# State space part: turning rows of X and B during the projection that forms them, with all copies on ScalarE

## What is computed

```python
xbc = silu(causal_dwconv(xbc, conv_w, conv_b))        # 4 taps, 4096 columns of h @ w_in
xs, Bm, Cm = split(xbc, (D_INNER, D_INNER + G * N))   # 2048 | 1024 | 1024 columns
dt = softplus(dt_raw + dt_bias)
X = xs * dt[..., None]
a_cs = cumsum(dt * A)
CB = einsum('bclgn,bcsgn->bcgls', Cc, Bc)
y_diag = einsum('bcgkls,bcsgkp->bclgkp', CB * Ldec, X)
states = einsum('bclgn,bcgkl,bclgkp->bcgkpn', Bc, exp(a_cs[..., -1:] - a_cs), X)
y_off = einsum('bclgn,bcgkpn,bcgkl->bclgkp', Cc, prev, exp(a_cs))
y = y_diag + y_off + d_skip[:, None] * xs
```

## Time and profile before

| | us |
|---|---|
| Median of 3 runs | 2085.98 |
| Lowest and highest | 2085.65 and 2087.79 |
| The profiled execution | 2083.6 |
| Its span in the profile | 2081.8 |
| TensorE busy | 1980.2 (95%) |
| VectorE busy | 1660.5 (80%) |
| ScalarE busy | 1303.8 (63%) |
| DMA | 498.76 MB, mean 240 GB/s |

### The profile page before, as it was taken

One profiled execution on the slowest core, in us unless ns is written; L12 is line 12 of the kernel. 1 busy time (PEld: TensorE's weight loads), 2 busy tenths in 40 slices (PEclk: granted clock), 3 DMA queues, 4 the chain that ended last, 5 costly groups with the idle time before them and its releaser, 6 DMA issues. The chain is left out here.

```text
span 2081.8 us, 28079 instructions
## 1 busy us (share of the span) xinstructions
PE 1980.2 (95%) x11165; PEld 1704.3 (82%) x11165; DVE 1660.5 (80%) x2110; ACT 1303.8 (63%) x1943; POOL 0.2 (0%) x4
## 2 busy tenths in 40 slices
PE   7879999998999999999999999989999999999999
PEld 4768788877778888888888888879888789989997
DVE  5876898677689989998999899978755756757884
ACT  3644444366587777787878787757564745536663
POOL 0000000000000000000000000000000000000000
PEclk9888999999999999999999999999999999989999
DMA  8625798731269989998999899845424443324553
GB/s 322 230 101 183 268 366 336 265 147 41 102 261 367 357 334 360 363 363 324 370 357 361 332 365 363 337 166 199 143 81 140 148 160 124 120 99 143 186 187 113
DMA packets 70809, 498.76 MB, mean 240 GB/s; under 512 B 8080, under 2 KB 8336, under 8 KB 11408
## 3 DMA queue, kind: packets, MB, share of 16 engines
q1 hardware_dynamic: 69952, 494.28, 64.1%
q10 hardware_dynamic: 720, 2.62, 0.3%
HBM read 495.82 MB, written 1.05 MB: 239 GB/s over the span
## 5 line engine op out<-in xcount | busy, mean ns | idle before, releaser
L345 DVE TENSOR_TENSOR wlo<-ring,whi 128x1024 fp32r<-128x1024 f32 (+1 forms) x845 | 1016.2, 1217 | 244.1 <-ACT whi L393 223.5
L393 ACT ACTIVATE whi<-ring 128x1024 fp32r<-128x1024 f32 (+1 forms) x845 | 884.8, 1054 | 480.8 <-PE ps L237 402.9
L237 PE MATMUL ps<-whi,hT 128*128 128x256 f32 (+2 forms) x944 | 318.0, 337 | 13.0 <-DVE hTl L299 4.3
L237 PE MATMUL ps<-wlo,hT 128*128 128x256 f32 (+2 forms) x944 | 312.8, 331 | 0.0
L237 PE MATMUL ps<-whi,hTl 128*128 128x256 f32 (+2 forms) x944 | 312.7, 331 | 0.0
L237 PE MATMUL ps<-whi,xg 128*128 128x512 f32 (+1 forms) x768 | 289.3, 377 | 1.4 <-DVE wlo L345 1.1
L237 PE MATMUL ps<-whi,xgl 128*128 128x512 f32 (+1 forms) x768 | 285.8, 372 | 0.0
L237 PE MATMUL ps<-wlo,xg 128*128 128x512 f32 (+1 forms) x768 | 285.5, 372 | 0.0
L237 PE MATMUL ps<-whi,hf 128*128 128x512 f32 x528 | 208.2, 394 | 4.8 <-DVE wlo L345 3.2
L237 PEld LDWEIGHTS ps<-whi,hT 128*128 128x128 f32 x944 | 183.3, 194 | 35.1 <-DVE wlo L345 7.4
L237 PE MATMUL ps<-wlo,hf 128*128 128x512 f32 x528 | 205.7, 390 | 0.0
(11 more groups left out here) (299 smaller groups left out, 2602.8 us busy)
## 6 DMA issues: line engine op xcount, KB each, us to landing
ring<-in_wstream SPq DMA_DIRECT2D x462, 1024.0 KB, 5.0
ring<-in_wstream SPq DMA_DIRECT2D x4, 832.0 KB, 5.2
modrow<-in_gates ACTq DMA_DIRECT2D x3, 512.0 KB, 6.9
ring<-in_wstream SPq DMA_DIRECT2D x6, 256.0 KB, 2.6
cst<-in_cst SPq DMA_DIRECT2D x1, 1028.0 KB, 7.7
x<-in_x SPq DMA_DIRECT2D x1, 1024.0 KB, 13.6
work<-in_bias ACTq DMA_DIRECT2D x2, 512.0 KB, 5.2
ring<-in_wstream SPq DMA_DIRECT2D x2, 512.0 KB, 3.8
```

Of the source, the lines that this page charges most:

```text
L237: i = self.e.matmul(out, lhsT, rhs, start=start, stop=stop, skip_group_check=True)
L345: i = self.e.tensor_tensor(K.wlo[:, q % NS, 0:cols], src, hi.bitcast(F32), ALU.subtract)
L393: i = self.e.activation(K.whi[:, q % NS, 0:cols], K.ring[:, m % RING, at:at + cols], ACT.Copy)
```

## The change

The ten groups of transposes no longer stand behind unit 0 of qkv0. They stand in `at_block`, ahead of blocks 7, 8, 11, 12, 15, 16, 19 and 20 (X: quarter n, chunk of tokens i, once silu of block 4n+3 is done) and 25 and 29 (B), in banks 6 and 7. All ten copies are made by ScalarE, in its iteration j behind the silu of block j-1. VectorE's four copies are gone. The wait of TensorE ahead of the states, and that of VectorE ahead of `XD`, name the new copies.

```diff
+SSD_TURNS = {7 + 4 * n + i: (n, i) for n in range(4) for i in range(2)} | {25: (4, 0), 29: (5, 0)}
+
+def row_bank(n, i):
+    return 6 + (i if n < 4 else n - 4)
+
+def ssd_turned(K, n, i):
+    return K.X[:, i, 512 * n:512 * n + 512] if n < 4 else K.Brow[:, 512 * (n - 4):512 * (n - 4) + 512]
...
+        if j in SSD_TURNS:
+            n, i = SSD_TURNS[j]
+            b = row_bank(n, i)
+            pe.take(b)
+            pe.wait_ge(K.act, ("xbc", "silu", 4 * n + 3))
+            for q in range(4):
+                pe.tr(K.ps[b][:, 128 * q:128 * q + 128], xbc[:, 4 * n + q, 128 * i:128 * i + 128], done=("row", n, i) if q == 3 else None)
+            pe.given(b, (K.act, ("row", n, i)))
     pe_cols(K, pe, "xbc", 32, "conv", ready(K, pe, "n1"), at_block=at_block)
     pe_project(K, pe, "qkv0", 0, 1, QKV0)
-    pe.wait_ge(K.act, ("xbc", "silu", 23))
-    for i in range(2):
-        for q0 in range(0, 16, 4):
-            b = next_bank(K, ("X", i, q0))
-            pe.take(b)
-            for q in range(4):
-                pe.tr(...)
-            pe.given(b, (K.dve if q0 % 8 else K.act, ("X", i, q0)))
-    for q0 in (0, 4):
...
     pe_project(K, pe, "qkv0", 1, 3, QKV0)
     pe.wait_ge(K.dve, "XS")
-    pe.wait_ge(K.act, ("B", 4))
+    pe.wait_ge(K.act, ("row", 5, 0))
...
+        if j in SSD_TURNS:
+            n, i = SSD_TURNS[j]
+            a.wait_ge(K.pe, ("row", n, i))
+            a.act(ssd_turned(K, n, i), K.ps[row_bank(n, i)][:, :], ACT.Copy, key=("row", n, i), own=False)
...
     act_project(K, a, "qkv0", 0, 1, QKV0, K.rows0)
-    for i in range(2):
-        for q0 in (0, 8):
-            a.wait_ge(K.pe, ("X", i, q0))
-            a.act(X[:, i, 128 * q0:128 * q0 + 512], ..., ACT.Copy, key=("X", i, q0), own=False)
-    for q0 in (0, 4):
...
     dve_project(K, v, "qkv0", 0, 1)
-    for i in range(2):
-        for q0 in (4, 12):
-            v.wait_ge(K.pe, ("X", i, q0))
-            v.copy(X[:, i, 128 * q0:128 * q0 + 512], ..., key=("X", i, q0), own=False)
-    v.wait_ge(K.act, ("X", 1, 8))
+    v.wait_ge(K.act, ("row", 3, 1))
     v.tt(heads(XD), heads(X[:, 0, :]), wide(dt[:, 0, :]), ALU.mult)
```

More of the change, by code:

```diff
@@ L2297, in at_block @@
             pe.given(4, (K.dve, "acs"))
+        if j in SSD_TURNS:
[6 more added lines that the diff above has]
+            pe.given(b, (K.act, ("row", n, i)))
     pe_cols(K, pe, "xbc", 32, "conv", ready(K, pe, "n1"), at_block=at_block)
     pe_project(K, pe, "qkv0", 0, 1, QKV0)
-    pe.wait_ge(K.act, ("xbc", "silu", 23))
-    for i in range(2):
-        for q0 in range(0, 16, 4):
-            b = next_bank(K, ("X", i, q0))
-            pe.take(b)
-            for q in range(4):
-                pe.tr(K.ps[b][:, 128 * q:128 * q + 128], xbc[:, q0 + q, 128 * i:128 * i + 128], done=("X", i, q0) if q == 3 else None)
-            pe.given(b, (K.dve if q0 % 8 else K.act, ("X", i, q0)))
-    for q0 in (0, 4):
[L2309 to L2313, removed]
     pe_project(K, pe, "qkv0", 1, 3, QKV0)
     pe.wait_ge(K.dve, "XS")
-    pe.wait_ge(K.act, ("B", 4))
+    pe.wait_ge(K.act, ("row", 5, 0))
     for g in range(8):
@@ L2383, in act_ssd @@
     act_project(K, a, "qkv0", 0, 1, QKV0, K.rows0)
-    for i in range(2):
-        for q0 in (0, 8):
-            a.wait_ge(K.pe, ("X", i, q0))
-            a.act(X[:, i, 128 * q0:128 * q0 + 512], K.ps[K.bank.get(("X", i, q0), 4)][:, :], ACT.Copy, key=("X", i, q0), own=False)
-    for q0 in (0, 4):
-        a.wait_ge(K.pe, ("B", q0))
-        a.act(Brow[:, 128 * q0:128 * q0 + 512], K.ps[K.bank.get(("B", q0), 4)][:, :], ACT.Copy, key=("B", q0), own=False)
     def steps(u):
@@ L2444, in dve_ssd @@
     dve_project(K, v, "qkv0", 0, 1)
-    for i in range(2):
-        for q0 in (4, 12):
-            v.wait_ge(K.pe, ("X", i, q0))
-            v.copy(X[:, i, 128 * q0:128 * q0 + 512], K.ps[K.bank.get(("X", i, q0), 4)][:, :], key=("X", i, q0), own=False)
-    v.wait_ge(K.act, ("X", 1, 8))
+    v.wait_ge(K.act, ("row", 3, 1))
     v.tt(heads(XD), heads(X[:, 0, :]), wide(dt[:, 0, :]), ALU.mult)
```

## The result

| | kernel before | with the change |
|---|---|---|
| Median | 2086.15 us (7 runs, 2083.93 to 2087.9) | 2077.97 us (7 runs, 2077.21 to 2084.18) |
| The profiled execution | 2083.6 us | 2078.14 us |
| Its span | 2081.8 us | 2076.3 us |
| Ratio | | 0.9967, 95% interval 0.9954 to 0.998 |

The changed kernel is 0.33% faster. The forecast had the sign, but the median lies 1.3 us under the range, and the ratio stands for 6.9 us (4.2 to 9.6) where 5.2 were forecast.

What follows compares the result with a forecast made beforehand. TensorE was taken to bound the kernel. Removing the turning's 10.16 us and adding 5.0 us for ten groups gave 5.2 us less: 2080.8 us against the median of 2085.98, range 2079.3 to 2084.3 us.

Steps and rivals of the forecast that it cites:

- What bounds: Whole kernel: TensorE, busy 95% of the span, is the limit; time counts only where it stands still or its work changes.
- What the turning costs: Stretch of transposes and copies between units 0 and 1 of qkv0: 10.16 us, all on TensorE's path.
- What a group costs: Four transposes placed between two blocks of xbc: 0.50 us of TensorE's time, 5.0 us for ten groups.
- the low end: Lowest price for a group, from two groups in one place amid matmuls: 0.44 us each, 4.4 us for ten.
- The copies: ScalarE's ten copies of 0.60 us in xbc: costed at nothing, covered by 18.0 us idle ahead of splits.
- The waits: TensorE's waits for silu ahead of groups in xbc: no cost expected, slack over 3 us ahead of block 7.
- The rival that copies set the pace: In xbc, each copy delays TensorE's next chunk by 0.60 us, 6.0 us lost, 2086.8 us; chance 0.17.
- XS: VectorE's second product of X, needed for the states: forecast 0.8 us early, and the next thing to be late.
- The slower rival: Clock falls to 1.2 GHz behind groups in xbc, 1.7 us each, up to 2097.8 us; chance 0.05 with other stalls.
- The range: Forecast bounds for the whole kernel's median, 2079.3 to 2084.3 us, with half a microsecond allowed for scatter of runs.

Runs made afterwards that it cites:

- the unchanged copies: The kernel before, run again with nothing changed, as a control: medians 2084.96 and 2085.0 us, ratios 1.0000 and 1.0001.

## Why the prediction was right or wrong

**What bounds.** This was right. TensorE's path is worth its full length: 15.5 us put on it cost 15.1, and 5.6 us put on it took the gain away.

**What the turning costs.** This was right: 10.16 us were forecast and 10.14 measured. The clock went back to 1.00 with the idle time, and no row of the place was under it.

**What a group costs.** Forecast 0.50 us, measured 0.43, 0.7 us for the ten. The step that failed is the sentence "No wait is in it". The four transposes from which the exit of 0.41 us was read stand behind a wait for VectorE's copy: the row itself says so (`[0.35 <-DVE wb L313]` in the earlier trace rows), and it is 0.66 us long, against 0.60 for four that follow matmuls directly. The run with early groups has both kinds at full clock, without a copy that the next matmul would wait for (timeline of PE):

```profile
1458.00 0.60 PE L256 MATMUL ps<-cst,wa 128*128 128x128 f32 x4
1458.35 0.36 PE L237 MATMUL ps<-hT,whi 128*128 128x256 f32 x1
1489.53 0.66 PE L256 MATMUL ps<-cst,wa 128*128 128x128 f32 x4 [1.97 <-ACT wa L375]
1489.94 0.36 PE L237 MATMUL ps<-hT,whi 128*128 128x256 f32 x1
```

The distance to the next matmul is 0.35 us in the first, and 0.41 behind a wait (0.38 to 0.41 in the four such groups at full clock). That is 0.06 of the 0.07 us. The rows of groups that follow matmuls without a wait gave 0.44 us, which I had put down as the low end because "one entry and one exit serve two groups". The doubled transposes show that there is no such price to share. Taking that row would have made the sum 5.8 us, which is what the place gives, and 2080.2 us.

**The copies.** They were costed at nothing, and they cost nothing, even doubled. The reason was half right: the idle time ahead of splits is the cover, but with the ten copies it rose by 2.6 us, where it was to fall by up to 6, since each group also makes ScalarE wait longer for TensorE. The rival that copies set the pace (0.17) is out.

**The waits.** The forecast was right that they cost nothing, but the reason was mis-sized. The prediction has "the slack is over 3 us", worked out for the first group; in the changed kernel it is 2.1 us, as silu of block 3 ends at 1404.15 and the group begins at 1406.22. ScalarE ends it 3.7 us behind the end of block 4 (1400.46), not 2, in part because it waits for VectorE's taps:

```profile
1403.73 0.42 ACT L375 ACTIVATE wa<-wa 128x256 f32<-128x256 f32 x1 [0.74 <-DVE wa L299]
```

With the early groups the same waits in TensorE's queue made xbc 24.8 us longer.

**XS.** It was forecast 0.8 us early and was 1.0 us early, so it was no gate.

**The clock in xbc.** The slower rival (0.05) did not come: xbc's clock is 1.00 in all profiles with groups at their place, with eight transposes in each as well. The Trainium skill ("TensorE: Matmul & The Clock Gate", Part 4: PE-mode transpose) says that full clock does not engage for transposes. In these runs a group did not take the clock from the matmuls behind it.

**The range.** This is what made the prediction miss. The step that failed is "I allow the range half a microsecond for that". Executions of one kernel differ by far more than the three that I had: 2076.8 to 2089.7 us in the 31 of the kernel before in the first set of experiments, 2074.5 to 2082.6 in 11 of the changed one. A median of seven moves by more than half a microsecond (an estimate: medians of seven drawn from those 31 scatter by 1.0 us, from those 11 by 1.1, as standard deviation). With 5.84 us from the place, the first median of 2085.98 would give 2080.1, inside the range; 2077.97 was measured. Five of the seven executions behind it lie between 2077.2 and 2078.2 and two at 2083.6 and 2084.2. Their mean is 2079.4, inside the range as well, so that the median fell outside is in part luck.

The ratio that 5.84 us make, 0.9972, is in each of the three intervals of the changed kernel (0.9954 to 0.998, 0.9954 to 0.9977, 0.9949 to 0.9977), though always in their upper half. The medians of the three sets differ by 8.2, 7.1 and 7.0 us, and by 6.4 where the unchanged copies (2084.96 and 2085.0) are taken. The means of all executions on record in each set differ by 6.8, 7.0 and 5.9 us, with 95% intervals of 2.5, 1.6 and 2.4 us to either side, so 5.84 is inside each. Whether what is left, some 0.1 to 1.2 us by the means, is chance, or the low-clock stretches come a little less often with an earlier arrival, the runs leave open; three profiles each show no difference (569.22 and 569.45 us).

## What to carry to other kernels

Where a full engine has a stretch of short dependent exchanges (fill a bank, wait for its copy), look for a place in which the same work can be strewn between long independent pieces: the copies then fall into time in which the other engine waits for the full one anyway. Place each piece so late that what it needs is done by a margin, for its wait blocks the whole queue: groups two to four blocks earlier turned 0.3% faster into 0.8% slower. Price such a piece from a row amid steady work, and look at each row from which a distance is read for a wait in front of it. And before a range is given for a gain of some tenths of a per cent, compare stretches that were not changed: the range must hold at least what they differ by between two executions.

## What the runs showed of the hardware

- A transpose of 128x128 fp32 amid matmuls costs 0.108 us of TensorE's time, with no price for changing over and back, while its row is 0.27 us long. Four that begin behind a wait take 0.03 to 0.06 us more up to the next matmul.
- A product of 128x256 with fp32 constants costs 0.43 us and leaves two rows; one with the rounded parts costs 0.12 us.
- The low-clock stretches behind the same idle times come and go between executions of one kernel: 17.2 to 27.8 us of 1.2 GHz in 567 to 571 us, for the same instructions, and the length follows.
- In the turning before the change the clock fell after 2.27 us of idle time and some shorter waits; in the same turning with four banks (1.40 and 0.42 us idle) it stayed at 1.00. The length of a wait alone does not tell: with the early groups the clock fell behind waits of 2.00, 2.06, 3.70 and 4.87 us, and stayed at 1.00 behind another of 2.06 and one of 1.97.
